# The recurrence of a two-block transformer kernel: the next round's decays and scaled operands made between the levels of this round's inverse, with its four rounds written out

## What is computed

```python
def step(state, inp):
    r_t, w_t, k_t, v_t, a_t, b_t = inp
    sa = jnp.einsum('bhvk,bhk->bhv', state, a_t)
    state = (state * w_t[:, :, None, :] + sa[..., None] * b_t[:, :, None, :]
             + v_t[..., None] * k_t[:, :, None, :])
    y_t = jnp.einsum('bhvk,bhk->bhv', state, r_t)
    return state, y_t
...
_, y = lax.scan(step, state0, xs)
```

## Time and profile before

| what | us |
|---|---|
| median of 3 runs | 2757.28 |
| lowest and highest run | 2750.9, 2760.48 |
| the profiled execution, device time | 2754.07 |
| its span, first to last instruction | 2752.1 |
| TensorE busy in the span | 2533.0 (92%) |
| VectorE, ScalarE, GpSimd busy | 1146.1, 952.1, 1000.8 |

### The profile page before, as it was taken

One profiled execution on the slowest core, in us unless ns is written; L12 is line 12 of the kernel. 1 busy time (PEld: TensorE's weight loads), 2 busy tenths in 40 slices (PEclk: granted clock), 3 DMA queues, 4 the chain that ended last, 5 costly groups with the idle time before them and its releaser, 6 DMA issues. The chain is left out here.

```text
span 2752.1 us, 38902 instructions
## 1 busy us (share of the span) xinstructions
PE 2533.0 (92%) x15170; PEld 1863.9 (68%) x15170; DVE 1146.1 (42%) x1593; ACT 952.1 (35%) x1367; POOL 1000.8 (36%) x495
## 2 busy tenths in 40 slices
PE   7999998999999899999899999999878899589996
PEld 5776776788877577777678887777577687233334
DVE  5443422565653622342256655343744513411113
ACT  4443432444433333343254442343422322211112
POOL 5221521444366232152244437642121442223330
PEclk9999999999999889999999999999999999699998
DMA  3111321222266111132122217422000221699992
GB/s 129 69 47 39 111 96 54 100 91 91 76 221 224 59 46 46 46 115 84 67 99 94 91 68 250 170 85 76 2 4 17 93 76 62 238 406 356 381 370 103
DMA packets 76284, 333.94 MB, mean 121 GB/s; under 512 B 17113, under 2 KB 21209, under 8 KB 51801
## 3 DMA queue, kind: packets, MB, share of 16 engines
q1 hardware_dynamic: 62336, 313.98, 30.8%
q0 software_dynamic: 13824, 18.19, 1.9%
HBM read 372.67 MB, written 16.78 MB: 142 GB/s over the span
## 5 line engine op out<-in xcount | busy, mean ns | idle before, releaser
L227 PE MATMUL bank<-dense_s_hi,dense_w_hi 128*128 128x512 f32 x672 | 267.0, 397 | 14.5 <-POOL dense_w_lo L702 8.9
L228 PE MATMUL bank<-dense_s_lo,dense_w_hi 128*128 128x512 f32 x672 | 261.9, 390 | 0.0
L229 PE MATMUL bank<-dense_s_hi,dense_w_lo 128*128 128x512 f32 x672 | 261.8, 390 | 0.0
L702 POOL TENSOR_TENSOR dense_w_lo<-weights,dense_w_hi 128x1024 fp32r<-128x1024 f32 x77 | 199.1, 2586 | 93.5 <-ACT dense_w_hi L671 90.6
L1497 DVE TENSOR_TENSOR hidden<-up_y 128x512 f32 x44 | 158.3, 3598 | 64.6 <-ACT up_y L1461 64.0
L229 PE MATMUL bank<-xn_r,weights_r 128*128 128x512 f32 x448 | 176.7, 394 | 0.0
L227 PEld LDWEIGHTS bank<-dense_s_hi,dense_w_hi 128*128 128x128 f32 x672 | 126.0, 188 | 55.3 <-POOL dense_w_lo L702 17.2
L1858 DVE SCALAR_TENSOR_TENSOR xn<-mix,xn 128x1024 f32<-128x1024 f32 x64 | 113.5, 1773 | 117.1 <-DMA mix<-in_modulation 106.0
L3075 PE MATMUL bank<-moe_weights,mix 128*64 128x512 f32 x320 | 143.8, 600 | 8.7 <-DMA experts_more_up<-in_experts_up,moe_more_up 8.5
L1474 POOL TENSOR_TENSOR up_w_lo<-weights,up_w_hi 128x2048 fp32r<-128x2048 f32 x22 | 101.5, 4616 | 126.7 <-ACT up_w_hi L1449 126.7
L227 PE MATMUL bank<-xn_r,mix_r 128*128 128x512 f32 x352 | 141.9, 403 | 5.5 <-DVE up_xn_lo_r L345 5.4
(11 more groups left out here) (707 smaller groups left out, 6140.4 us busy)
## 6 DMA issues: line engine op xcount, KB each, us to landing
weights<-in_w_up SPq DMA_DIRECT2D x44, 1024.0 KB, 4.8
moe_weights<-in_experts_up SPq DMA_DIRECT2D x40, 1024.0 KB
mix<-in_modulation SPq DMA_DIRECT2D x64, 512.0 KB, 5.2
weights<-in_w_xattn SPq DMA_DIRECT2D x24, 1024.0 KB, 4.8
weights<-in_experts_up SPq DMA_DIRECT2D x24, 1024.0 KB
weights<-in_w_down SPq DMA_DIRECT2D x44, 512.0 KB, 4.0
moe_weights<-in_experts_down SPq DMA_DIRECT2D x40, 512.0 KB, 10.3
weights<-in_w_attn SPq DMA_DIRECT2D x8, 1536.0 KB, 6.6
```

What stands on the lines that cost most here:

```text
L227: nc.tensor.matmul(out, left.hi, right.hi, start=first, stop=False)
L228: nc.tensor.matmul(out, left.hi, right.lo, start=False, stop=False)
L229: return nc.tensor.matmul(out, left.lo, right.hi, start=False, stop=last)
L702: nc.gpsimd.tensor_tensor(w[b].lo[:, :], units.rows(b, 0, D, 0, D), w[b].hi[:, :], ALU.subtract).then_inc(w_split, 1)
```

## The change

On ScalarE, VectorE and GpSimd the head of round i+1 is issued inside round i. `ar` and `ep` get two buffers per chunk, used in turn (`w.ars`, `w.eps`), and 12 x 256 instead of 6 x 256 columns are reserved for buffers. The exponentials of chunk 0 come behind ScalarE's copies of level 1, those of chunk 1 behind level 2, both `epv` behind level 3. VectorE makes `dl` of both chunks behind level 1, `bt` and `kt` of chunk 0 behind level 2 and of chunk 1 behind level 3, and the two halves of `ar` of both chunks behind level 4. GpSimd copies the values behind its twelve masks. TensorE's waits for `y_ready`, `s_added` and `v_copied` move from ahead of its first product to ahead of the transposition of the values. The four rounds are written out (`range` instead of `Fori`), with constants in the waits; `after` (a wait that is left out where its count is not positive) exists already. The increments of `passed` go.

```diff
         places = [slot[:, :] for slot in g.ring.slots] + [flat(g.memn), flat(g.square), g.std[:, :], g.rstd[:, :],
-                                                          sb("own", [P, 6 * UNIT])[:, :]]
+                                                          sb("own", [P, 12 * UNIT])[:, :]]
...
-            w.ar = carve(PAIRS, 2, C)
+            w.ars = [carve(PAIRS, 2, C) for _ in TWO]
...
-            w.dl, w.en, w.ep, w.epv = (carve(PAIRS, C) for _ in range(4))
+            w.dl, w.en, w.epv = (carve(PAIRS, C) for _ in range(3))
+            w.eps = [carve(PAIRS, C) for _ in TWO]
...
-            with act.Fori(0, ROUNDS) as i:
-                for p, w in enumerate(chunks):
-                    act.wait_ge(s_ready, 2 * i + p)
-                    nc.scalar.activation(w.en, now(rw.L, i, p), ACT.Exp, scale=-rate).then_inc(w.exps_ready, 1)
-                    nc.scalar.activation(w.ep, now(rw.L, i, p), ACT.Exp, scale=rate).then_inc(w.exps_ready, 1)
-                    act.wait_ge(w.diff_ready, i + 1)
-                    nc.scalar.activation(w.epv, w.dl, ACT.Exp, scale=rate).then_inc(w.exps_ready, 1)
+            def inverse_decay(i, p, w):
+                after(act, w.scaled, 4 * i)
+                nc.scalar.activation(w.en, now(rw.L, i, p), ACT.Exp, scale=-rate).then_inc(w.exps_ready, 1)
+
+            def decay(i, p, w):
+                after(act, s_ready, 2 * i - 3 + p if i >= 2 else 0)
+                nc.scalar.activation(w.eps[i % 2], now(rw.L, i, p), ACT.Exp, scale=rate).then_inc(w.exps_ready, 1)
+
+            def decay_ahead(i, w):
+                act.wait_ge(w.diff_ready, i + 1)
+                nc.scalar.activation(w.epv, w.dl, ACT.Exp, scale=rate).then_inc(w.exps_ready, 1)
+
+            for p, w in enumerate(chunks):
+                inverse_decay(0, p, w)
+                decay(0, p, w)
+                decay_ahead(0, w)
+            for i in range(ROUNDS):
                 for p, w in enumerate(chunks):
                     act.wait_ge(w.pairs_done, 4 * i + 3)
                     nc.scalar.activation(w.bk.rearrange("p a b n -> p (a b n)"), g.bank[(2, 7)[p]][:, :], ACT.Copy).then_inc(w.tokens_read, 1)
@@ -2331,46 +2342,62 @@
                     for w in chunks:
                         act.wait_ge(w.w_done, LEVELS * i + l + 1)
                         nc.scalar.activation(w.Wt, wide(w.w_bank), ACT.Copy).then_inc(w.w_ready, 1)
+                    if i + 1 < ROUNDS and l <= 2:
+                        inverse_decay(i + 1, l - 1, chunks[l - 1])
+                        decay(i + 1, l - 1, chunks[l - 1])
+                    if i + 1 < ROUNDS and l == 3:
+                        for w in chunks:
+                            decay_ahead(i + 1, w)
                 for p, w in enumerate(chunks):
                     act.wait_ge(w.rhs_done, i + 1)
                     nc.scalar.activation(w.rhs, wide(7), ACT.Copy).then_inc(w.rhs_ready, 1)
                     act.wait_ge(w.u_done, i + 1)
                     nc.scalar.activation(w.U, wide(4), ACT.Copy).then_inc(w.u_ready, 1)
-                    act.wait_ge(w.y_done, i + 2)
+                    act.wait_ge(w.y_done, i + 1)
                     nc.scalar.activation(now(rw.y, i, p), wide((5, 3)[p]), ACT.Copy).then_inc(w.y_ready, 1)
 
         @block.gpsimd
         def _(pool):
-            with pool.Fori(0, ROUNDS) as i:
+            def copy_values(i):
                 for p, w in enumerate(chunks):
-                    pool.wait_ge(s_ready, 2 * i + p)
+                    after(pool, w.pairs_done, 4 * i)
                     nc.gpsimd.tensor_copy(w.vt, now(rec.v, i, p)).then_inc(w.v_copied, 1)
+            copy_values(0)
+            for i in range(ROUNDS):
                 for w in chunks:
                     pool.wait_ge(w.pairs_read, 2 * i + 1)
                     nc.gpsimd.tensor_tensor(w.al[:, 0, :, :], w.Mb[:, :, 0, :], spread(level(0)), ALU.mult).then_inc(w.level_ready, 1)
                 for l in range(1, LEVELS):
                     for w in chunks:
                         nc.gpsimd.tensor_tensor(w.al[:, l, :, :], w.Mb[:, :, 0, :], spread(level(l)), ALU.mult).then_inc(w.level_ready, 1)
+                if i + 1 < ROUNDS:
+                    copy_values(i + 1)
 
         @block.vector
         def _(dve):
+            def difference(i, p, w):
+                after(dve, w.exps_ready, 3 * i)
+                nc.vector.tensor_tensor(w.dl, now(rw.L, i, p), now(rec.ell, i, p), ALU.subtract).then_inc(w.diff_ready, 1)
+
+            def scale_keys(i, p, w):
+                after(dve, w.pairs_done, 4 * i - 1)
+                dve.wait_ge(w.exps_ready, 3 * i + 2)
+                nc.vector.tensor_tensor(w.bt, now(rw.b, i, p), w.en, ALU.mult).then_inc(w.scaled, 1)
+                nc.vector.tensor_tensor(w.kt, now(rec.k, i, p), w.en, ALU.mult).then_inc(w.scaled, 1)
+
+            def scale_queries(i, p, w):
+                after(dve, w.y_done, i - 1)
+                nc.vector.tensor_tensor(w.ars[i % 2][:, :, 1, :], now(rec.r, i, p), w.eps[i % 2], ALU.mult).then_inc(w.scaled, 1)
+                dve.wait_ge(w.exps_ready, 3 * i + 3)
+                nc.vector.tensor_tensor(w.ars[i % 2][:, :, 0, :], now(rw.nkk, i, p), w.epv, ALU.mult).then_inc(w.scaled, 1)
+
             nc.vector.memset(S[0][:, :, :], 0.0).then_inc(s_added, 1)
-            dve.sem_inc(s_ready, 1)
-            for w in chunks:
-                dve.sem_inc(w.y_done, 1)
-                dve.sem_inc(w.y_ready, 1)
-            with dve.Fori(0, ROUNDS) as i:
-                for p, w in enumerate(chunks):
-                    dve.wait_ge(s_ready, 2 * i + p)
-                    nc.vector.tensor_tensor(w.dl, now(rw.L, i, p), now(rec.ell, i, p), ALU.subtract).then_inc(w.diff_ready, 1)
-                for p, w in enumerate(chunks):
-                    dve.wait_ge(w.exps_ready, 3 * i + 2)
-                    dve.wait_ge(w.y_done, i + 1)
-                    nc.vector.tensor_tensor(w.bt, now(rw.b, i, p), w.en, ALU.mult).then_inc(w.scaled, 1)
-                    nc.vector.tensor_tensor(w.kt, now(rec.k, i, p), w.en, ALU.mult).then_inc(w.scaled, 1)
-                    nc.vector.tensor_tensor(w.ar[:, :, 1, :], now(rec.r, i, p), w.ep, ALU.mult).then_inc(w.scaled, 1)
-                    dve.wait_ge(w.exps_ready, 3 * i + 3)
-                    nc.vector.tensor_tensor(w.ar[:, :, 0, :], now(rw.nkk, i, p), w.epv, ALU.mult).then_inc(w.scaled, 1)
+            for p, w in enumerate(chunks):
+                difference(0, p, w)
+            for p, w in enumerate(chunks):
+                scale_keys(0, p, w)
+                scale_queries(0, p, w)
+            for i in range(ROUNDS):
                 for w in chunks:
                     for j, m in enumerate((w.Mb, w.Mk)):
                         dve.wait_ge(w.pairs_done, 4 * i + j + 1)
@@ -2389,13 +2416,22 @@
                             nc.vector.tensor_tensor(w.M, wide(w.z_bank), w.M, ALU.add).then_inc(w.inverse_step, 1)
                         dve.wait_ge(w.zt_done, (LEVELS - 1) * i + l)
                         nc.vector.tensor_tensor(w.MT, wide(w.zt_bank), w.MT, ALU.add).then_inc(w.inverse_step, 1)
+                    if i + 1 < ROUNDS:
+                        if l == 1:
+                            for p, w in enumerate(chunks):
+                                difference(i + 1, p, w)
+                        if l in (2, 3):
+                            scale_keys(i + 1, l - 2, chunks[l - 2])
+                        if l == 4:
+                            for p, w in enumerate(chunks):
+                                scale_queries(i + 1, p, w)
                 for p, w in enumerate(chunks):
                     dve.wait_ge(w.s_done, i + 1)
                     dve.wait_ge(s_added, 2 * i + p + 1)
-                    after = S[1 - p][:, :, :]
-                    nc.vector.tensor_tensor(after, wide(6), S[p][:, :, :], ALU.add).then_inc(s_added, 1)
+                    later = S[1 - p][:, :, :]
+                    nc.vector.tensor_tensor(later, wide(6), S[p][:, :, :], ALU.add).then_inc(s_added, 1)
                     dve.wait_ge(s_added, 2 * i + p + 2)
-                    nc.vector.tensor_tensor(after, after, w.ep[:, :, C - 1:C].broadcast_to([P, PAIRS, C]), ALU.mult).then_inc(s_ready, 1)
+                    nc.vector.tensor_tensor(later, later, w.eps[i % 2][:, :, C - 1:C].broadcast_to([P, PAIRS, C]), ALU.mult).then_inc(s_ready, 1)
 
...
-            with pe.Fori(0, ROUNDS) as i:
-                for w in chunks:
-                    pe.wait_ge(w.y_ready, i + 1)
+            for i in range(ROUNDS):
                 for p, w in enumerate(chunks):
+                    ar = w.ars[i % 2]
                     pe.wait_ge(w.scaled, 4 * i + 4)
-                    pe.wait_ge(w.v_copied, i + 1)
-                    pe.wait_ge(s_added, 2 * i + 1)
-                    pe.sem_inc(passed, 1)
                     for j, left in enumerate((w.bt, w.kt)):
                         if p == 1:
```

(19 more changed lines are left out.)

## The result

| | before | after |
|---|---|---|
| median, us (runs) | 2754.64 (4) | 2732.56 (4) |
| lowest and highest run | 2750.9, 2760.48 | 2730.52, 2734.58 |
| profiled execution, its span | 2754.07, 2752.1 | 2730.52, 2728.7 |

The changed kernel is faster: the ratio is 0.9911 with a 95% interval of 0.9896 to 0.9927, some 24 us; the two medians of the table lie 22.1 us apart. The forecast of 2739 lay 6.4 us above the measured 2732.56.

What follows compares the result with a forecast made beforehand. TensorE was taken to bound the recurrence stage, idle at round borders awaiting VectorE's scaled operands. 13.6 + 4.8 + 0.3 - 0.3 - 1.7 = 16.7 us off 2754.07 gives 2737.4, put at 2739 for the median; range 2731 to 2749.

Steps and rivals of the forecast that it cites:

- The three borders: Between rounds, TensorE's wide products follow the last outputs directly instead of waiting for scaled operands: 13.6 us gained.
- The clock behind them: Chunk 0's wide products behind each border run at the higher clock: 1.6 us a border, 4.8 us gained.
- The start: At the stage's start, ScalarE's wait for VectorE's register work goes with the loop: 0.3 us gained.
- What is put between the levels: Work inserted between levels fits idle times, except VectorE's `dl` beside GpSimd's masks, making `M` late: 0.3 us lost.
- inserted-work rival: VectorE's four inserted groups each delay `M` and `MT` by 0.76 us, 9.1 us in all: 2748; chance 0.06.
- Four rounds written out: TensorE's straight code makes levels of rounds 2 to 4 longer, like round 1's: 1.7 us lost.
- code-supply rival: Without border pauses, TensorE's code blocks in the levels each come 0.9 us late, 9 us: about 2746; chance 0.13.
- slower one: All 34 of the stage's code blocks come 0.9 us late and stop TensorE: 2762.4, some 2764 as median; chance 0.03.
- the prediction's own signs: Stage some 17 us shorter, levels of rounds 2 to 4 18.2 to 19.2 us; gain under 8 or over 20 wrong.

Runs made afterwards that it cites:

- loop experiment: Changed kernel with TensorE back in a loop of two rounds a pass, with register waits and the increments of `passed`; median 2741.97 us, ratio 0.9932.
- idle-product experiment: Kernel before with TensorE's rounds written out and 36 idle products put at each border between rounds; median 2764.95 us, ratio 1.0024.

## Why the prediction came out as it did

*The three borders*, taken as 13.6: right, 14.0 from start to start. The next late thing was as far off as the step said. The loop experiment adds what the step did not know: the jump would have kept 3.4 of each 4.6 us by itself, had only the order been changed.

*The clock behind them*, 4.8: right, 4.85, and shown by itself in the idle-product experiment. *The start*, 0.3: TensorE's first product comes 5.03 us after the last of the stage before it instead of 5.63, and the first wide products are 0.3 us shorter.

*What is put between the levels*, -0.3: the overlap with GpSimd came as described (0.88 and 0.94), and `M` came 0.26 us late, within the 0.1 to 0.5 foreseen; VectorE's idle time ahead of it fell to nothing, and not to 0.6. But the next product did not lack it, so it cost nothing. The inserted-work rival falls with it.

*Four rounds written out*, -1.7: this is where the prediction failed, by a term that it did not have. The diff's last sentence, the increments of `passed` go, I priced at nothing and never set beside the pauses. Without them levels and tails are 5.6 us shorter in the new order and 5.9 in the old (112.2 to 106.2). The written-out rounds by themselves, with the increments kept, made levels and tails together 1.1 us longer with all engines written out and 3.2 with TensorE alone. The 1.7 is of that size by luck: the step put it into the levels, which did not grow (73.9 and 74.6 us against 74.5), and the tails did. Its reason was wrong too: I read the pauses as what straight code brings, and took round 1's longer levels as what all rounds would become. They go with code that arrives late, but only where the increments stand behind the waits; the old order without increments has 17.59 to 17.68 in straight code. Instead of -2.0 for this term and the one above, the stage shows +4.9, which is 6.9 of the 8.2 us by which its 24.9 exceed the sum of 16.7. The code-supply rival and the slower one fell with the same step. By the prediction's own signs, a stage some 17 us shorter, levels of 18.2 to 19.2 us and a gain of at most 20, it is wrong.

Some of its sums were off besides. 2.6 plus 3 x 2.4 is 9.8 and not 9, and three borders of 0.9 us are 2.7 a round and 10.7 in all, so that the upper end of the code supply should have been 9.8 to 10.7. The slower rival decides from (18.7 + 3.6) / 0.9, about 25 late blocks, and not 20. Neither moves the forecast.

*The profile against the median*: the stage is 24.9 us shorter and begins 1.8 us earlier, yet the span is only 23.4 us less. The remaining 3.3 us went behind the stage, which took 622.8 us in the profiled execution of before, 626.0 after, and 624.5 to 630.4 in the experiments' executions, in no order that follows the change. It is spread between executions.

What is open: why an increment behind its waits makes code arrive late, where as many increments ahead of the waits don't. That the pauses come with such increments is shown, in both orders, and that they end 1.2 to 1.6 us after a packet of code. That TensorE's sequencer, held at these instructions, asks for its next code too late is an explanation that fits, and no run shows it.

## What to carry to other kernels

When an engine is dense with work of 0.03 us an instruction, look at what stands between its waits and its work. Here an increment behind the waits put them on a separate instruction; that cost 0.1 to 0.2 us at each wait for ScalarE in the tail, and pauses of up to 1.5 us that go with late code. The same increments ahead of the waits cost nearly nothing. Make what the next round needs ahead of time where the other engines idle, and take the loop off the dense engine in the same step, since either the late operand or the jump alone keeps the pause and the low clock behind it. And price every line of a diff, also the one that counts nothing anybody waits for.

## What was not expected of the hardware

- The jump of TensorE's loop cost 3.4 us of idle time with all operands ready, and 1.7 us more by the clock.
- An increment behind a wait for ScalarE's copy adds 0.1 to 0.2 us to it: 0.57 with constants, 0.67 at chunk 0's solve where the wait is on the loop's counter, against 0.47. 135 more semaphore instructions, nearly all without a wait, added 0.6 us to the stage.
- 26 pauses of TensorE in straight stretches, in six kernels, each ended 1.2 to 1.6 us after a packet of instructions had ended.
- An idle border of 2.9 us left the clock low behind it in round 2 and at 1.00 in rounds 3 and 4 of one kernel, and low behind every border of another; one of 0.7 us left it at 1.00 each time.
